# Second attention of a two-block transformer kernel: the grouped heads taken in pairs, input units placed ahead of them, weight splits placed behind their steps

## The reference, cut to what matters

```python
proj = einsum('bsd,de->bse', rmsnorm(x, attn_norm_g), w_in)      # 1024 x 2304
qa, ka, va, qb, kb, vb = split(proj, ...)
qa, ka = axial_rope(rmsnorm(qa)), axial_rope(rmsnorm(ka))        # 8 query heads, 2 key heads of 64
out_a = softmax(qa @ ka.T / 8) @ va                              # 4 query heads to a key head
s = qb @ kb.T / 8 + bias                                         # 4 heads, 2 parts c of 64 each
attn = softmax(s[:, 0]) - lam * softmax(s[:, 1])
out_b = rmsnorm(attn @ vb) * (1 - lambda_init)                   # 4 heads, values of 128
x = x + concat(out_a, out_b) @ w_out                             # 1024 x 1024
x = x + square(relu(rmsnorm(x) @ w_up)) @ w_down
```

## Time and profile before

| | before |
|---|---|
| median of 3 runs | 1355.21 us (1354.40 to 1356.15) |
| the profiled execution | 1354.38 us |
| its span in the profile | 1352.2 us |
| PE busy | 1297.1 us (96%) |
| DVE busy | 1023.0 us (76%) |
| ACT busy | 856.6 us (63%) |
| DMA | 319.31 MB, mean 236 GB/s |
| mean granted PE clock | 0.98 |

### The profile page before, as it was taken

How to read it: one execution, slowest core, us unless ns; L and a number is a source line. 1 busy time by engine, 2 the same in 40 slices (tenths; PEclk the granted TensorE clock), 3 DMA queues, 4 the chain that set the end, 5 groups by cost and what they waited for, 6 DMA issues and landing times.

```text
span 1352.2 us, 18794 instructions
## 1 busy us (share of the span) xinstructions
PE 1297.1 (96%) x6058; PEld 1060.4 (78%) x6058; DVE 1023.0 (76%) x1483; ACT 856.6 (63%) x1257; POOL 31.9 (2%) x44
## 2 busy tenths in 40 slices
PE   8999999999988999999999999999998887999998
PEld 6878888887676888888888888888876665788887
DVE  7486555567677999999999999999995645555554
ACT  6555444457554878878787878788784554554442
POOL 0000000001000000000000000000000010000000
PEclk9999999999898999999999999999998888999999
DMA  9645555553153988889797989898994221355540
GB/s 368 253 157 186 187 187 186 186 175 136 63 166 115 374 326 346 325 353 374 301 372 300 365 306 375 318 367 325 352 352 156 95 94 39 119 185 194 179 156 32
DMA packets 46585, 319.31 MB, mean 236 GB/s; under 512 B 5232, under 2 KB 6512, under 8 KB 8272
## 3 DMA queue, kind: packets, MB, share of 16 engines
q1 hardware_dynamic: 44704, 316.40, 62.4%
q10 hardware_dynamic: 1728, 2.10, 0.5%
q0 software_dynamic: 112, 0.26, 0.1%
HBM read 316.64 MB, written 2.10 MB: 236 GB/s over the span
## 4 chain that ended last, share of the span: by engine, by line
PE 81%; DVE 10%; ACT 4%; issue 3%; DVEq 0%; DMA 0%; SPq 0%; POOL 0%; ACTq 0%
PE bank L366 24%; PE bank L368 24%; PE bank L367 24%; DVE wl L1582 4%; PE bank L762 3%; PE bank L430 2%; ACT wh L1023 2%; DVE x L2107 2%; PE bank L402 1%; PE bank L866 1%; PE bank L624 1%; PE bank L889 1%; PE bank L623 1%; ACT act L1467 1%; DVE xtl L1602 0%
## 5 line engine op out<-in xcount | busy, mean ns | idle before, releaser
L1582 DVE TENSOR_TENSOR wl<-raw,wh 128x1024 fp32r<-128x1024 f32 x598 | 713.8, 1218 | 191.4 <-ACT wh L1023 182.4
L1023 ACT ACTIVATE wh<-raw 128x1024 fp32r<-128x1024 f32 x598 | 630.6, 1058 | 294.4 <-PE bank L368 289.6
L366 PE MATMUL bank<-wh,xth 128*128 128x512 f32 (+2 forms) x1154 | 461.7, 400 | 5.7 <-DVE xtl L1602 2.8
L368 PE MATMUL bank<-wh,xtl 128*128 128x512 f32 (+2 forms) x1154 | 450.5, 390 | 0.0
L367 PE MATMUL bank<-wl,xth 128*128 128x512 f32 (+2 forms) x1154 | 450.1, 390 | 0.0
L366 PEld LDWEIGHTS bank<-wh,xth 128*128 128x128 f32 x1154 | 219.8, 190 | 53.7 <-issue 4.3
L368 PEld LDWEIGHTS bank<-wh,xtl 128*128 128x128 f32 x1154 | 219.2, 190 | 46.3
L367 PEld LDWEIGHTS bank<-wl,xth 128*128 128x128 f32 x1154 | 220.0, 191 | 41.5
L366 PE MATMUL bank<-wh,hth 128*128 128x512 f32 x472 | 186.5, 395 | 0.0
L368 PE MATMUL bank<-wh,htl 128*128 128x512 f32 x472 | 185.1, 392 | 0.0
L367 PE MATMUL bank<-wl,hth 128*128 128x512 f32 x472 | 184.7, 391 | 0.0
(11 more groups left out here) (297 smaller groups left out, 747.4 us busy)
## 6 DMA issues: line engine op xcount, KB each, us to landing
raw<-weights_dram SPq DMA_DIRECT2D x299, 1024.0 KB, 4.9
x<-x_dram SPq DMA_DIRECT2D x2, 512.0 KB, 6.2
wide<-bias_scratch ACTq DMA_DIRECT2D x8, 128.0 KB, 2.6
out_dram<-x SPq DMA_DIRECT2D x4, 256.0 KB, 2.1
fixed<-fixed_dram SPq DMA_DIRECT2D x1, 536.0 KB, 10.4
bias_scratch<-act ACTq DMA_DIRECT2D x2, 256.0 KB, 8.6
bias_scratch<-hbuf ACTq DMA_DIRECT2D x2, 256.0 KB, 15.1
rows<-rows_dram POOLq DMA_DIRECT2D x1, 256.0 KB, 3.9
```

Of the source, the lines that this page charges most:

```text
L366: mm(o, lh, wh[:, wi, sl], start=start, stop=False)
L368: return mm(o, ll, wh[:, wi, sl], start=False, stop=stop)
L1023: A(wh[:, c % SPLIT, 0:n], raw[:, (c // 2) % RAW, (c % 2) * UNIT:(c % 2) * UNIT + n], ACT.Copy).then_inc(hi_done, 1)
L1582: V.tensor_tensor(wl[:, c % SPLIT, 0:n], raw[:, (c // 2) % RAW, (c % 2) * UNIT:(c % 2) * UNIT + n], f32(wh[:, c % SPLIT, 0:n]), ALU.subtra ...
```

## The change

The grouped heads are taken in four pairs instead of one by one: pair j is head j, whose key head lies on the lower half of the partitions, and head j + 4, on the upper half. `scores_a(j)` makes both heads' scores, alternating between the halves, into banks 4 and 5. `turn_a(j, s)` stays one step per head, but into banks 7 and 6. `copy_a(j, s)` copies into `act` instead of `hbuf`. `values_a(j)` makes both heads' values, alternating between the lower and upper 64 partitions of bank 6. Since other heads now share a 128-row group of the outputs, the rows of `w_out_2` are laid out in that order when the weight stream is packed. `row_max_a(j)` reduces both banks and scales once; `weigh_a(j)` multiplies a head's 512 columns in one instruction instead of two of 256.

In PE's order, units 10 to 12 of the input projection come ahead of the first grouped heads' turning, and later units stand between the steps of a pair. The queries and keys of the second kind are transposed earlier, through banks 0 to 3. `turn_ob` always goes through bank 6, which `turn_b` uses too, so new waits tie the two (`b_pT`, `ob_l`), and its source rows live in three rotating places of `xn`. `scores_b` loops over the query block outside and the part c inside. On ACT and DVE, splits of weights are put off behind the steps of heads, and `evac_in2` waits for its own unit. `queries_a` comes ahead of the sums of squares of the queries. The diff, cut (indentation shortened):

```diff
+        ob_turned = bank[6][:, 0:256]
+        def ob_rows(t, h):
+    at = 640 + h % 3 * P
+    return xn[:, t, at:at + P]
...
-    def scores_a(h):
-        if h >= 2:
-            pe.wait_ge(sem("head_e"), 2 * NH + 2 * h - 2)
-        r0 = (h // 4) * 64
+    def scores_a(j):
+        if j >= 1:
+            pe.wait_ge(sem("head_e"), 2 * NH + 4 * j)
         for qb in range(2):
-            last = mm(bank[4 + h % 2][:, qb * 256:(qb + 1) * 256], hT2[r0:r0 + 64, h % 4, qb * P:(qb + 1) * P],
-                      hT2[r0:r0 + 64, 4, :], start=True, stop=True)
+            for s in range(2):
+                last = mm(bank[4 + s][:, qb * 256:(qb + 1) * 256], hT2[s * 64:s * 64 + 64, j, qb * P:(qb + 1) * P],
+                          hT2[s * 64:s * 64 + 64, 4, :], start=True, stop=True)
         last.then_inc(sem("head_S"), 1)
-    def turn_a(h):
-        pe.wait_ge(sem("head_p"), NH + h + 1)
-        if h >= 1:
-            pe.wait_ge(sem("head_pT"), NH + h)
+    def turn_a(j, s):
+        pe.wait_ge(sem("head_p"), NH + 2 * j + 2 - s)
+        if j >= 1:
+            pe.wait_ge(sem("head_pT"), NH + 2 * j - s)
+            if s == 0:
+                pe.wait_ge(sem("head_ol"), NH + j)
         for kb in range(2):
             for qb in range(2):
-                last = nc.tensor.transpose(bank[6][:, kb * 256 + qb * P:kb * 256 + (qb + 1) * P],
-                                           ebuf[:, h % 2, qb * 256 + kb * P:qb * 256 + (kb + 1) * P], ident)
+                last = nc.tensor.transpose(bank[6 + s][:, kb * 256 + qb * P:kb * 256 + (qb + 1) * P],
+                                           ebuf[:, s, qb * 256 + kb * P:qb * 256 + (kb + 1) * P], ident)
         last.then_inc(sem("head_PT"), 1)
-    def values_a(h):
-        pe.wait_ge(sem("head_pT"), NH + h + 1)
-        if h >= 2 and h % 2 == 0:
-            pe.wait_ge(sem("head_ol"), NH + h // 2)
-        r0 = (h % 2) * 64
-        v0 = 640 + (h // 4) * 64
+    def values_a(j):
+        pe.wait_ge(sem("head_pT"), NH + 2 * j + 2)
         for kb in range(2):
-            last = mm(bank[7][r0:r0 + 64, 0:256], act[:, kb, v0:v0 + 64],
-                      hbuf[:, h % 2, kb * 256:(kb + 1) * 256], start=(kb == 0), stop=(kb == 1))
+            for s in range(2):
+                last = mm(bank[6][s * 64:s * 64 + 64, 0:256], act[:, kb, 640 + s * 64:704 + s * 64],
+                          act[:, s, kb * 256:(kb + 1) * 256], start=(kb == 0), stop=(kb == 1))
         last.then_inc(sem("head_O"), 1)
...
+        else:
+            pe.wait_ge(sem("head_ol"), NH + 4)
+        if h >= 2:
+            pe.wait_ge(sem("ob_l"), h - 1)
...
-    def turn_ob(h, o):
+    def turn_ob(h):
         pe.wait_ge(sem("ob_c"), 2 * h + 2)
+        pe.wait_ge(sem("b_pT"), min(h + 2, NB2))
+        if h >= 1:
+            pe.wait_ge(sem("ob_l"), h)
         for t in range(NT):
-            last = nc.tensor.transpose(o[:, t * P:(t + 1) * P], xn[:, t, h * P:(h + 1) * P], ident)
+            last = nc.tensor.transpose(ob_turned[:, t * P:(t + 1) * P], ob_rows(t, h), ident)
         last.then_inc(sem("ob_T"), 1)
...
     pairs_turned(bank[5], xn, 0, 2)
     pairs_turned(bank[6], xn, 256, 2)
+    in2(10)
     pe.wait_ge(sem("h2T_c"), 3)
     scores_a(0)
+    in2(11)
+    in2(12)
     scores_a(1)
-    in2(10)
-    for h in range(NH):
-        turn_a(h)
-        if h + 2 < NH:
-            scores_a(h + 2)
-        values_a(h)
-        if h + 11 < 18:
-            in2(h + 11)
-        if h == 5:
-            pe.wait_ge(sem("b_ready"), 1)
-            pe.wait_ge(sem("in2_c"), 8)
-            pairs_turned(bank[2], act, 768, 2)
-            pairs_turned(bank[3], act, 1024, 2)
+    turn_a(0, 1)
+    turn_a(0, 0)
+    in2(13)
+    in2(14)
+    turn_a(1, 1)
+    values_a(0)
+    pe.wait_ge(sem("b_ready"), 1)
+    pe.wait_ge(sem("in2_c"), 6)
+    pairs_turned(bank[0], act, 768, 2)
+    pairs_turned(bank[1], act, 1024, 2)
+    scores_a(2)
+    turn_a(1, 0)
+    in2(15)
+    values_a(1)
+    pe.wait_ge(sem("h2T_c"), 5)
+    in2(16)
+    scores_a(3)
+    turn_a(2, 1)
+    turn_a(2, 0)
+    in2(17)
+    values_a(2)
     pe.wait_ge(sem("b_ready"), 2)
+    pe.wait_ge(sem("in2_c"), 8)
+    pairs_turned(bank[2], act, 1280, 2)
+    pairs_turned(bank[3], act, 1536, 2)
+    turn_a(3, 1)
+    turn_a(3, 0)
+    pe.wait_ge(sem("h2T_c"), 7)
     pe.wait_ge(sem("head_e"), 2 * NH + 2 * NH)
-    pairs_turned(bank[4], act, 1280, 2)
-    pairs_turned(bank[5], act, 1536, 2)
+    scores_b(0)
     pe.wait_ge(sem("in2_c"), 10)
     out2(0)
-    pe.wait_ge(sem("h2T_c"), 7)
-    scores_b(0)
+    scores_b(1)
+    values_a(3)
     out2(1)
-    scores_b(1)
     turn_b(0)
+    scores_b(2)
+    values_b(0)
+    turn_b(1)
     out2(2)
-    values_b(0)
-    scores_b(2)
-    turn_b(1)
+    turn_ob(0)
+    scores_b(3)
+    values_b(1)
     out2(3)
-    values_b(1)
-    scores_b(3)
     turn_b(2)
-    pe.wait_ge(sem("b_nm"), NB2)
-    turn_ob(0, bank[4])
+    turn_ob(1)
     values_b(2)
-    turn_ob(1, bank[5])
     turn_b(3)
+    values_b(3)
+    turn_ob(2)
     out2(4)
-    values_b(3)
-    pe.wait_ge(sem("b_pT"), NB2)
-    turn_ob(2, bank[6])
+    turn_ob(3)
     out2(6, (0,))
-    turn_ob(3, bank[4])
     out2(5)
     out2(6, (1,))
+    pe.wait_ge(sem("b_nm"), NB2)
     turn_half("mlp2", 0, 4)
...
+        sc.wait_ge(unit_used, U_IN2 + min(4 * n + 4, 18))
...
+    def copy_a(j, s):
+        sc.wait_ge(sem("head_PT"), NH + 2 * j + 2 - s)
+        if j >= 1:
+            sc.wait_ge(sem("head_O"), NH + j)
+        A(act[:, s, 0:512], bank[6 + s][:, :], ACT.Copy).then_inc(sem("head_pT"), 1)
...
+    follow(U_IN2 + 10, 1, 0)
     exps_a(0)
+    evac_in2(2)
+    sc.wait_ge(sem("in2_c"), 6)
+    sc.wait_ge(sem("a_red"), 2)
+    square_b(0)
+    follow(U_IN2 + 11, 1, 0)
+    copy_a(0, 1)
+    copy_a(0, 0)
     exps_a(1)
...
     follow(U_OUT2, 1, 0)
-    copy_b(0)
+    out_hi_a(3)
     exps_b(1)
     follow(U_OUT2 + 1, 1, 0)
+    copy_b(0)
     squares_b(0)
     copy_b(1)
     exps_b(2)
+    ob_hi(0)
     follow(U_OUT2 + 2, 1, 0)
     squares_b(1)
+    exps_b(3)
     copy_b(2)
-    exps_b(3)
-    ob_hi(0, bank[4])
+    follow(U_OUT2 + 3, 1, 0)
...
+        dv.wait_ge(sem("a_sq"), 4 - 2 * n)
...
+        dv.wait_ge(sem("in2_c"), 4)
...
+    def weigh_a(j):
+        for s in (1, 0):
+            dv.wait_ge(sem("head_e"), 2 * NH + 4 * j + 4 - 2 * s)
+            link(V.reciprocal(small[:, 76 + 2 * s:78 + 2 * s], small[:, 72 + 2 * s:74 + 2 * s]))
+            p = ebuf[:, s, :].rearrange("p (q n) -> p q n", q=2)
+            by = small[:, 76 + 2 * s:78 + 2 * s][:, :, None].to_broadcast((P, 2, 256))
+            V.tensor_tensor(p, p, by, ALU.mult).then_inc(sem("head_p"), 1)
...
-    follow(U_IN2, 4, 0)
+    follow(U_IN2, 3, 0)
     dv.wait_ge(sem("a_sq"), 2)
     sums(0, 0, 2, asq[:, :, 512:640], 1.0 / HD, EPS)
-    follow(U_IN2 + 4, 2, 0)
+    follow(U_IN2 + 3, 1, 0)
     keys_a()
-    follow(U_IN2 + 6, 2, 0)
+    follow(U_IN2 + 4, 3, 0)
+    queries_a()
     dv.wait_ge(sem("a_sq"), 4)
     sums(1, 4, 8, asq[:, :, 0:512], 1.0, HD * EPS)
-    queries_a()
-    follow(U_IN2 + 8, 2, 0)
+    follow(U_IN2 + 7, 3, 0)
     dv.wait_ge(sem("lam_e"), 1)
     link(V.tensor_tensor(lam[:, 4:5], lam[:, 3:4], lam[:, 2:3], ALU.subtract))
...
+    first = w["w_out_2"][0][0:AQ].reshape(2, 4, HD, D).transpose(1, 0, 2, 3).reshape(AQ, D)
+    mixed = np.concatenate([first, w["w_out_2"][0][AQ:]], 0)
     for u, (pair, n) in enumerate(WO_UNITS):
-        pairs(U_OUT2 + u, w["w_out_2"][0][256 * pair:256 * (pair + 1), n * WIDE:(n + 1) * WIDE])
+        pairs(U_OUT2 + u, mixed[256 * pair:256 * (pair + 1), n * WIDE:(n + 1) * WIDE])
...
```

More of the change, by code:

```diff
@@ L896, in scores_b @@
                     pe.wait_ge(sem("b_nm"), h)
-                for c in range(2):
-                    for qb in range(2):
+                for qb in range(2):
+                    for c in range(2):
                         last = mm(bank[4 + c][:, qb * 256:(qb + 1) * 256],
@@ L2321, in _ @@
             row_max_a(0)
+            follow(U_IN2 + 10, 1, 0)
+            weigh_a(0)
             row_max_a(1)
-            weigh_a(0)
+            dv.wait_ge(sem("b_sq"), 2)
+            sums(2, 20, 8, bsq[:, :, 0:512], 1.0, HD * EPS)
+            follow(U_IN2 + 11, 1, 0)
             weigh_a(1)
-            for h in range(NH):
-                if h + 2 < NH:
-                    row_max_a(h + 2)
-                if h % 2:
-                    out_lo_a(h // 2)
-                if h + 10 < 18:
-                    follow(U_IN2 + h + 10, 1, 0)
-                if h + 2 < NH:
-                    weigh_a(h + 2)
-                if h == 2:
-                    dv.wait_ge(sem("b_sq"), 2)
-                    sums(2, 20, 8, bsq[:, :, 0:512], 1.0, HD * EPS)
-                if h == 4:
-                    dv.wait_ge(sem("h2_rs"), 3)
-                    scaled_b(768, 20)
-                if h == 6:
-                    dv.wait_ge(sem("b_sq"), 4)
-                    sums(3, 36, 8, act[:, :, 2304:2816], 1.0 / HD, EPS)
```

(44 more changed lines are left out.)

132 lines of the change are left out of this document (57 added, 75 removed).

## The result

The changed kernel takes **1320.4 us** (median of 4 runs, 1316.7 to 1321.2) against 1354.8 before (median of 4 runs too, one more than stood ahead of the prediction): ratio 0.973, 95% interval 0.971 to 0.975. The prediction was 1320.0, range 1315 to 1331.

The account below looks back on a forecast made before the run. PE was taken as the bound, losing time to waits and half clock in the second attention. Passes -4.2, -4.0, -0.5, idle -16.3 and half clock -10.6 gave -35.6, taken as -35: 1320.0 us, range 1315 to 1331.

Parts of the forecast that it names:

- Items 1 to 3: Grouped heads on PE: scores in pairs -4.2 us, values in pairs -4.0, fewer changes of block shape -0.5.
- rival of columns that don't overlap: Values in pairs gain nothing because the two column halves don't run side by side: +4.0, 1324 us; chance 0.16.
- Item 4: Second attention's queries: turning ahead of the sums, split behind the copy; PE's 3.1 us wait goes to 0.
- Item 5: Grouped heads: two units (5.5 us) between a pair's scores and first turning cover about 4 us; costed at nothing.
- Item 6: Second kind's queries and keys: the wait for scaled keys goes from 3.8 to about 0.2 us.
- Item 7: Second kind's heads: splits leave three of four heads' path; 7.2 + 1.5 us of waits go, except item 8's.
- Item 8: New waits on bank 6, shared by `turn_ob` and `turn_b`, at the second kind's heads: 3.1 us.
- Item 9: Splits of weights put off on ACT and DVE hold up nothing; costed at nothing.
- Half clock: PE's time at 1.2 GHz in the second attention: 12.5 us before, 1.9 left behind item 8's waits, -10.6.
- ACT and DVE as the bound: Rival: busy over 73% of 78 us, they cause six 1 us waits plus half clock: +9.7, 1329 or 1330; chance 0.14.
- The clock stays down: Rival: denser packed blocks and transposes keep PE at 1.2 GHz all through the stretch: +34, 1389 us; chance 0.02.
- It doesn't do what it says: Rival: PE's waits only move and packing alone is left, -4 to 0, about 1353 us; chance 0.04.

Follow-up runs that it names:

- scores_alone: The changed kernel with PE waiting for the lower half's scores before it starts the upper half's; 1323.5 us.
- values_alone: The changed kernel with PE waiting for the values on the lower half of the columns before it starts the upper half's; 1324.6 us.
- queries_late: The changed kernel with ACT's split ahead of the copy of the queries, and one more split and the sums ahead of DVE's turning; 1324.0 us.
- split_first: The changed kernel with DVE's splits ahead of the mixing for all four heads of the second kind; 1327.1 us.
- undone: The changed kernel with lower and upper halves one after another, queries late, keys early, no units before the first turnings, DVE's and ACT's splits first; 1353.6 us.
- all_waits: The changed kernel with the edits of queries_late and split_first, and the first two turnings ahead of units 11 and 12, packing kept; 1336.4 us.
- changed_again: The changed kernel measured once more, unedited, beside another version on the same chip; 1320.6 us.

## Why the prediction was right

- **Items 1 to 3, the passes.** Foreseen -8.7. A scores block of 8 takes 1.07 us and a values block 1.01, start to start, which is 4.1 + 4.0 = 8.1 less than the blocks before; scores_alone and values_alone each show their overlap by itself. Item 3's 0.5 for fewer changes of shape is shown by no run. Right, and the rival of columns that don't overlap (1324) is out.
- **Item 4, the queries.** Foreseen: ready 0.2 us before PE's unit 9 ends. In the changed kernel the last turning piece starts at 1053.04 and takes 1.29, and PE begins the transposes at 1054.52: 0.2 us. queries_late brought back the 3.1.
- **Item 5, the cover.** Costed at nothing, with two units (5.5 us) over a chain of 4: no wait in the trace, and 4.1 us without them.
- **Item 6, the keys.** 3.8 to 0.2 foreseen; no wait over 0.1 now, and 3.9 when their transposes go ahead again.
- **Item 7, the splits.** 8.7 us foreseen away but for item 8, and they are. That the splits did it is shown in part: DVE's ahead of the mixing bring 3.8 us of waits and 3.2 of half clock in the new order. The largest wait before, 3.3 us at `turn_b(0)`, had no unit to cover it between `scores_b(1)` and the turning, and now has one; item 7 doesn't name this, and with the splits put back the wait there is 0.6 (split_first) or none (undone). How the 7.2 us divide between DVE's splits, ACT's order and PE's stays open.
- **Item 8, the ring.** 3.1 us foreseen, 3.4 seen (0.7, 1.4, 0.9, and 0.4 at head 0), with the largest at `turn_b(3)` for the low part of an output, as said. Its working had only ACT's split on that path, which costs 0.3, and not DVE's, which costs 0.9; and the last wait is for the scaled output, which ended 0.1 us behind the copy that was named.
- **Item 9, the splits put off.** Costed at nothing, and no wait of PE for `wh` or `wl` is in the list of waits.
- **Idle time.** 20.1 to 3.6, foreseen 3.8. Of the 3.8, about 0.5 was for the MLP's norm, whose 0.4 us lie behind the stretch, before and after the change: the ring took 3.4 where 3.1 stood, and the errors nearly cancel.
- **Half clock.** This term was off twice, and the errors nearly cancelled. The work at 2.4 GHz was worked out as 71.7 and is 73.1; with 8.7 of passes added back (8.1 by the blocks), the kernel before had 81.8 us of work and 11.1 of half clock, not 12.5. And the changed kernel's stretch has none, not 1.9. So -11.1 where -10.6 stood. The rule of 0.62 us for each us of waits held roughly as a mean (10.4 / 15.5 = 0.67 in undone, but 5.6 / 12.1 = 0.46 in all_waits), not at one place (0.4 to 1.2).
- **ACT and DVE as the bound** (1329). They are busy 73% and 76% of the stretch, and PE waits for them in five places over 0.1 us, 3.4 us in all, where six of 1 us more were supposed. Out.
- **The clock stays down** (1389). 1.00, in a stretch in which 88 of PE's 433 records are transposes. The Trainium skill (TensorE: Matmul & The Clock Gate, Part 4) says that full clock does not engage for transposes, and by that rule this case was weighed; it is not borne out here, where transposes stand between matmuls. The prediction also put the time in 64-row and 64-column blocks and transposes at a third of the stretch of 1.00 before; by the earlier trace rows a head's are 2.59 us, from one turning at 1070.66 to the next, which the trace has at 1076.12, 5.46 us, so nearly half, which spoke still more against this case.
- **It doesn't do what it says** (1353). The waits did not move elsewhere: 16.5 of the 20.1 us are gone. Out.
- **The sum** was -35.6, taken as -35, and -36.3 came in the stretch; 2.1 went back ahead of it. Its own figures, 1319.4 and the 0.8 to the median, give 1320.2 where it has 1320.0. That the total came out at 1320.4 owes something to these 2.1 us.

## What to carry to other kernels

Where an in-order engine bounds the kernel and idles 18% of a stretch, sort the waits by what each chain waits for and set work that is ready ahead of it: here that was worth 16 us of waits and 11 of half clock, more than the 8 us of passes saved by filling both halves of the array. Price half clock with the waits, as a mean over many, with a range of its own. Compare an undone version with the old kernel wait by wait and not by its total: taking work away from one place in a new order can open a wait that the old order never had, as the 3.8 us at the first turning in undone. And measure a change of a few us by the stretch between two fixed instructions, not by the whole time.

## What was not expected of the hardware

The clock falls in code that no kernel here changes, and not always alike. Between 330 and 440 us the changed kernel had

```profile
330.00:440.00 110.00, 97.02 (x467) 75.45 (x466) 76.15 (x195) 55.81 (x119) 6.13 (x6) 0.89 0.28 99
```

and values_alone

```profile
330.00:440.00 110.00, 96.78 (x490) 76.79 (x489) 80.05 (x200) 59.97 (x124) 6.14 (x6) 0.94 0.30 107
```

467 matmuls against 490 in the same time, at 0.89 against 0.94; the kernel before had 0.92. With it the start of the second attention moved: 1054.5 to 1056.2 us in the profiles with 0.89, 1053.5 with 0.91, 1052.1 to 1052.5 with 0.92, 1050.5 to 1051.4 with 0.94. That is 5 us of 1320, larger than most of the single edits here. The runs of one kernel differ by 2 to 7 us, and their time goes with their mean clock (changed_again: 1320.9 us at 0.988, 1317.6 at 0.991), so this may be why; it may also be why queries_late shows 3.6 us more time than the changed kernel but 4.9 more stretch. What sets it off there was not tried.
